# One core, fp32r matmuls in high and low parts: a merged matmul of 512 columns in the up pass, and sums of halves on VectorE

## The reference

```
u = rms_norm(h, norm_mlp_g)
h = h + square(relu(u @ w_mlp_up)) @ w_mlp_down     # w_mlp_up 2048 x 8192, w_mlp_down 8192 x 2048
out = rms_norm(h, norm_final_g)
```

## Time and profile before

| | |
|---|---|
| time, median of 3 runs | 2653.86 us (2652.83 to 2655.21) |
| profiled execution | 2654.28 us, its span 2652.6 us |
| PE busy | 98% |
| DVE, ACT, POOL busy | 63%, 44%, 17% |
| up pass, pairs 1 to 31 | 1386.9 to 2011.8 us |
| longest waits of PE in the up pass | one of 9.3 us at its start |

### The profile page before, as it was taken

How to read it: one execution, slowest core, us unless ns; L and a number is a source line. 1 busy time by engine, 2 the same in 40 slices (tenths; PEclk the granted TensorE clock), 3 DMA queues, 4 the chain that set the end, 5 groups by cost and what they waited for, 6 DMA issues and landing times. The chain is left out here.

```text
span 2652.6 us, 37285 instructions
## 1 busy us (share of the span) xinstructions
PE 2595.1 (98%) x14068; PEld 2253.3 (85%) x14068; DVE 1658.5 (63%) x1673; ACT 1154.6 (44%) x1437; POOL 460.9 (17%) x321
## 2 busy tenths in 40 slices
PE   7999999999999999999989999999999899999998
PEld 6888878888888888888879999999998788888886
DVE  5436844433233332342377788777878889999996
ACT  4333354312233322232355556556555455455555
POOL 1000010000000000000002223322332344344343
PEclk9999999999999999999989999999999999999999
DMA  5222322222322222234335565565568865545651
GB/s 173 92 82 80 107 87 97 95 95 80 95 79 79 80 95 95 95 111 137 132 111 179 195 216 183 183 211 198 178 199 323 242 242 203 174 181 217 237 206 80
DMA packets 247374, 394.39 MB, mean 149 GB/s; under 512 B 8832, under 2 KB 156880, under 8 KB 238864
## 3 DMA queue, kind: packets, MB, share of 16 engines
q1 hardware_dynamic: 240848, 373.97, 41.6%
q0 software_dynamic: 5520, 14.16, 2.1%
q10 hardware_dynamic: 944, 5.42, 0.5%
HBM read 326.28 MB, written 67.11 MB: 148 GB/s over the span
## 5 line engine op out<-in xcount | busy, mean ns | idle before, releaser
L1050 DVE TENSOR_TENSOR wlo<-raw,whi 128x2048 fp32r<-128x2048 f32 (+1 forms) x113 | 258.1, 2284 | 542.2 <-ACT whi L643 542.1
L1550 PE MATMUL stream<-uhi,whi 128*128 128x512 f32 (+1 forms) x1312 | 511.3, 390 | 0.8 <-ACT rx L715 0.8
L1551 PE MATMUL stream<-ulo,whi 128*128 128x512 f32 (+1 forms) x1312 | 507.7, 387 | 0.0
L1552 PE MATMUL stream<-uhi,wlo 128*128 128x512 f32 (+1 forms) x1312 | 507.4, 387 | 0.0
L643 ACT CAST whi<-raw 128x2048 fp32r<-128x2048 f32 (+1 forms) x113 | 215.3, 1906 | 534.9 <-PE stream L1552 533.9
L1550 PEld LDWEIGHTS stream<-uhi,whi 128*128 128x128 f32 (+1 forms) x1312 | 245.4, 187 | 52.6 <-issue 2.6
L1552 PEld LDWEIGHTS stream<-uhi,wlo 128*128 128x128 f32 (+1 forms) x1312 | 245.3, 187 | 50.3
L1551 PEld LDWEIGHTS stream<-ulo,whi 128*128 128x128 f32 (+1 forms) x1312 | 245.4, 187 | 49.5 <-issue 1.0
L605 POOL TENSOR_TENSOR hh<-hh,dn_tmp 128x512 f32<-128x512 f32 x116 | 221.5, 1929 | 352.5 <-ACT dn_tmp L969 352.5
L1818 PE MATMUL stream<-shi,uwhi 128*128 128x256 f32 x896 | 255.1, 285 | 9.3 <-DVE slo L1325 9.3
L1819 PE MATMUL stream<-slo,uwhi 128*128 128x256 f32 x896 | 254.7, 284 | 0.0
(11 more groups left out here) (258 smaller groups left out, 5142.0 us busy)
## 6 DMA issues: line engine op xcount, KB each, us to landing
raw<-in_w_in SPq DMA_DIRECT2D x80, 1024.0 KB, 5.1
d<-in_w_mlp_down SPq DMA_DIRECT2D x64, 1024.0 KB, 8.5
dsum<-sums_d SPq DMA_DIRECT2D x56, 1024.0 KB, 8.7
up_a<-in_w_mlp_up SPq DMA_DIRECT2D x32, 1024.0 KB, 6.3
up_b<-in_w_mlp_up SPq DMA_DIRECT2D x32, 1024.0 KB, 8.6
sums_d<-hhi SPq DMA_DIRECT2D x32, 896.0 KB, 6.0
sums_d<-hlo SPq DMA_DIRECT2D x32, 896.0 KB, 7.8
raw<-in_w_out SPq DMA_DIRECT2D x16, 1024.0 KB, 5.1
```

Of the source, the lines that this page charges most:

```text
L1050: V.tensor_tensor(wlo[slot][:, 0:width], raw[slot][:, 0:width], whi[slot][:, 0:width].bitcast(F32), ALU.subtract).then_inc(s.lo_ready, 1)
L1550: T.matmul(dst, ah, bh, start=first and k == 0, stop=False)
L1551: T.matmul(dst, ah, bl, start=False, stop=False)
L1552: ins = T.matmul(dst, al, bh, start=False, stop=last and k == n - 1)
```

## The change

The high and the low part of each activation sum now lie in one tile `ssum[q]` with a dimension of two. For each block the high weights are multiplied with both parts in one matmul of 512 columns into a whole bank: the left half gets high x high, the right half high x low. The low weights are multiplied with the high part, 256 columns, into the left half. So a state is now the sum of the two halves of its bank. ACT copies the right half (counted in `up_right`), and DVE adds the left half to the copy (the new function `whole`, counted in `up_snap`). `hid_out` adds the right half in a second operation that waits for the first (`up_half`). c21 is copied without relu, and ACT applies the relu in place in `hid_act`, ahead of the square, which waits for it.

The queue of DVE in a pair becomes: hid_out(0), add 0, whole(U3 of the pair before), uwlo 0, add 1, uwlo 1, hid_out(2), add 2, uwlo 2, whole(c21 of the pair before), uwlo 3, whole(P1), add 3, uwlo 4, whole(Q5), uwlo 5, whole(U2), uwlo 6, hlo.

```diff
 
     HALF = S // 2
     hs = [at(f"hs{k}", 190 + 7 * k, [P, 7, HALF], F32) for k in range(2)]
-    sum_at = [(112, 119), (126, 133), (176, 183), (48, 80), (56, 88), (64, 96), (72, 104), (32, 39)]
-    shi = [at(f"shi{k}", a, [P, 7, HALF], F32R) for k, (a, _) in enumerate(sum_at)]
-    slo = [at(f"slo{k}", b, [P, 7, HALF], F32R) for k, (_, b) in enumerate(sum_at)]
+    sums_near = {k: at(f"sums{k}", kb, [P, 2, 7, HALF], F32R) for k, kb in ((0, 112), (1, 126), (2, 176), (7, 32))}
+    sums_far = at("sums_far", 48, [P, 2, 4, 8, HALF], F32R)
+    ssum = [sums_near[k][:] if k in sums_near else sums_far[:, :, k - 3, 0:7] for k in range(8)]
+    shi, slo = ([v[:, c] for v in ssum] for c in range(2))
     up_a = [at("up_a0", 0, [P, 8, 256], F32), at("up_a1", 144, [P, 8, 256], F32)]
     up_b = [at("up_b0", 8, [P, 8, 256], F32), at("up_b1", 152, [P, 8, 256], F32)]
     up_e = at("up_e", 140, [P, 8, P], F32)
...
             i = 4 * g + u
             n = 7 * i
             _, _, _, _, parts = up_parts(u)
-            a, c = up_bank(u, 0)[:, 0:HALF], up_bank(u, 1)[:, 0:HALF]
-            a_old = up_bank(u + 1, 0)[:, 0:HALF]
+            a, c = up_bank(u, 0)[:, HALF:S], up_bank(u, 1)[:, HALF:S]
+            a_old = up_bank(u + 1, 0)[:, HALF:S]
             for j in range(7):
                 act.wait_ge(s.up_mm, n + j + 1)
                 if j == 1 and not first:
                     act.wait_ge(s.up_c, 3 * i)
-                    nc.scalar.copy(snap["U3"][:], a_old).then_inc(s.up_snap, 1)
+                    nc.scalar.copy(snap["U3"][:], a_old).then_inc(s.up_right, 1)
                 if j == 3 and not first:
-                    nc.scalar.activation(c21[:], a_old, ACT.Relu).then_inc(s.up_snap, 1)
+                    nc.scalar.copy(c21[:], a_old).then_inc(s.up_right, 1)
                 if j == 4:
                     act.wait_ge(s.up_c, 3 * i + 1)
-                    nc.scalar.copy(snap["P1"][:], a).then_inc(s.up_snap, 1)
+                    nc.scalar.copy(snap["P1"][:], a).then_inc(s.up_right, 1)
                 if j == 5:
                     act.wait_ge(s.up_c, 3 * i + 3)
-                    nc.scalar.copy(snap["Q5"][:], c).then_inc(s.up_snap, 1)
+                    nc.scalar.copy(snap["Q5"][:], c).then_inc(s.up_right, 1)
                 if j == 6:
                     act.wait_ge(s.up_c, 3 * i + 2)
-                    nc.scalar.copy(snap["U2"][:], a).then_inc(s.up_snap, 1)
+                    nc.scalar.copy(snap["U2"][:], a).then_inc(s.up_right, 1)
 
                 if j < len(hooks):
                     hooks[j]()
...
             act.wait_ge(s.up_c, 3 * i + 6)
             nc.scalar.activation(up_out[:, :, 0:HALF], up_out[:, :, 0:HALF], ACT.Relu).then_inc(s.up_relu, 1)
             act.wait_ge(s.up_snap, 5 * i + 5)
+            nc.scalar.activation(c21[:], c21[:], ACT.Relu).then_inc(s.up_relu, 1)
             if begun:
                 act.wait_ge(s.hs_add, 4 * i)
+            act.wait_ge(s.up_relu, 2 * i + 2)
             nc.scalar.activation(h21[:], c21[:], ACT.Square).then_inc(s.up_sq, 1)
-            act.wait_ge(s.up_relu, i + 1)
             if begun:
                 act.wait_ge(s.hs_sp[u % 2], 64 * g + 32 * ((u - 2) // 2 + 1))
             nc.scalar.activation(hraw[:, 0:7:3], up_out[:, :, 0:HALF], ACT.Square).then_inc(s.up_sq, 1)
...
                     act.wait_ge(s.dn_mm, 14 * st + m + 1)
                 if first and m == 1:
                     act.wait_ge(s.up_c, 3 * PAIRS)
-                    nc.scalar.copy(snap["U3"][:], up_bank(3, 0)[:, 0:HALF]).then_inc(s.up_snap, 1)
+                    nc.scalar.copy(snap["U3"][:], up_bank(3, 0)[:, HALF:S]).then_inc(s.up_right, 1)
                 if first and m == 3:
-                    nc.scalar.activation(c21[:], up_bank(3, 0)[:, 0:HALF], ACT.Relu).then_inc(s.up_snap, 1)
+                    nc.scalar.copy(c21[:], up_bank(3, 0)[:, HALF:S]).then_inc(s.up_right, 1)
                 if m == 2 and not first:
                     dn_out(g - 1 + n, 1 - n, 4)
                 if m == 4 and not first:
...
 
         def sum_lo(k):
             dve.wait_ge(s.st_hi, k + 1)
-            V.tensor_tensor(slo[k][:], hs[k % 2][:], shi[k][:].bitcast(F32), ALU.subtract).then_inc(s.st_lo, 1)
+            V.tensor_tensor(slo[k], hs[k % 2][:], shi[k].bitcast(F32), ALU.subtract).then_inc(s.st_lo, 1)
 
         def out_sums(i):
             dve.wait_ge(s.h_in, 16 * i + 16)
...
                     if not isinstance(n, int) or n:
                         dve.wait_ge(s.up_lo, n)
                     add(0, up_e[:], b11, b12)
+                    if not first:
+                        whole(i - 1, 4, u - 1)
                 if j == 1:
                     dve.wait_ge(s.up_b[u % 2], loaded)
                     dve.wait_ge(s.up_lo, n + 1)
...
                 if j == 2:
                     add(2, b12, b12, b22)
                 if j == 4:
+                    whole(i, 0, u)
                     dve.wait_ge(s.up_lo, n + 2)
                     add(3, up_e[:], b11, b21)
                 if j < len(hooks):
                     hooks[j]()
                 k = (7 * u + j) % 4
+                if j >= 5:
+                    whole(i, j - 4, u)
+                if j == 3 and not first:
+                    whole(i - 1, 6, u - 1)
                 dve.wait_ge(s.up_hi, n + j + 1)
                 V.tensor_tensor(uwlo[k][:], parts[j], uwhi[k][:].bitcast(F32), ALU.subtract).then_inc(s.up_lo, 1)
                 if j == 6 and not first:
...
 
         def hid_out(i, u, j):
 
+            dve.wait_ge(s.up_mm, 7 * i + 8 + j)
+            x, part, op = ((0, "P1", ALU.add), None, (1, "U2", ALU.subtract))[j]
+            b = up_bank(u, 3 + j)
+            dve.wait_ge(s.up_snap, 5 * i + {0: 1, 2: 4}[j])
             if j == 0:
-                dve.wait_ge(s.up_mm, 7 * i + 8)
-                dve.wait_ge(s.up_snap, 5 * i + 1)
                 dve.wait_ge(s.up_sq, 2 * i + 2)
-                V.tensor_tensor(up_out[:, 0, 0:HALF], up_bank(u, 3)[:, 0:HALF], snap["P1"][:], ALU.add).then_inc(s.up_c, 1)
-            else:
-                dve.wait_ge(s.up_mm, 7 * i + 10)
-                dve.wait_ge(s.up_snap, 5 * i + 4)
-                V.tensor_tensor(up_out[:, 1, 0:HALF], up_bank(u, 5)[:, 0:HALF], snap["U2"][:], ALU.subtract).then_inc(s.up_c, 1)
+            V.tensor_tensor(up_out[:, x, 0:HALF], b[:, 0:HALF], snap[part][:], op).then_inc(s.up_half, 1)
+            if j == 2:
                 V.tensor_tensor(up_out[:, 2, 0:HALF], snap["Q5"][:], snap["U3"][:], ALU.subtract).then_inc(s.up_c, 1)
+            dve.wait_ge(s.up_half, 2 * i + j // 2 + 1)
+            V.tensor_tensor(up_out[:, x, 0:HALF], up_out[:, x, 0:HALF], b[:, HALF:S], ALU.add).then_inc(s.up_c, 1)
+
+        def whole(i, k, u):
+
+            part = (snap["P1"], snap["Q5"], snap["U2"], None, snap["U3"], None, c21)[k][:]
+            dve.wait_ge(s.up_right, 5 * i + {0: 1, 1: 2, 2: 3, 4: 4, 6: 5}[k])
+            V.tensor_tensor(part, up_bank(u, k)[:, 0:HALF], part, ALU.add).then_inc(s.up_snap, 1)
 
         def hid_lo(i):
             dve.wait_ge(s.hs_hi, i + 1)
...
                     dve.wait_ge(s.dn_b21, 16 * st + 16)
                     dve.wait_ge(s.dn_lo, 14 * st + 3 + hf)
                     add(3, dn_e[hf][:], b11, b21)
+                if first and m in (1, 3):
+                    whole(PAIRS - 1, m + 3, 3)
                 dve.wait_ge(s.dn_hi, 14 * st + m + 1)
                 V.tensor_tensor(dlo[m % 7][:], parts[j], dhi[m % 7][:].bitcast(F32), ALU.subtract).then_inc(s.dn_lo, 1)
                 if first and m == 1:
...
                 pe.wait_ge(s.up_lo, n + j + 1)
                 if j in (2, 4, 5, 6):
                     pe.wait_ge(s.up_snap, 5 * i + {2: 1, 4: 3, 5: 2, 6: 4}[j])
-                dst = up_bank(u, j)[:, 0:HALF]
+                dst = up_bank(u, j)
+                both = dst[:].rearrange("p (c n) -> p c n", c=2)
                 opens = j in (0, 1, 3)
                 for q in range(KP):
-                    wh, wl, sh, sl = uwhi[k][:, q], uwlo[k][:, q], shi[q][:, j], slo[q][:, j]
-                    T.matmul(dst, wh, sh, start=opens and q == 0, stop=False, skip_group_check=not opens)
-                    T.matmul(dst, wh, sl, start=False, stop=False, skip_group_check=not opens)
-                    ins = T.matmul(dst, wl, sh, start=False, stop=q == KP - 1, skip_group_check=not opens)
+                    wh, wl, hl, sh = uwhi[k][:, q], uwlo[k][:, q], ssum[q][:, :, j], shi[q][:, j]
+                    if q:
+                        T.matmul(dst[:, 0:HALF], wl, sh, start=False, stop=False, skip_group_check=True)
+                    ins = T.matmul(both, wh, hl, start=opens and q == 0, stop=q == KP - 1, skip_group_check=True)
+                    if q == 0:
+                        T.matmul(dst[:, 0:HALF], wl, sh, start=False, stop=False, skip_group_check=True)
                 ins.then_inc(s.up_mm, 1)
 
         for u in range(4):
```

(4 more changed lines are left out.)

## The result

The changed kernel takes 2703.4 us in the median of four runs (2702.45 to 2704.29); the kernel before, on the same chip, 2653.35 us (2652.62 to 2655.21). The ratio is 1.0185 with a 95% interval of 1.0172 to 1.0198: 50 us slower, where 42 were forecast. The profiled execution has a span of 2701.7 us, 49.1 more than before.

What follows compares the result with a forecast made beforehand. TensorE (20.16 us per pair) and a DVE-ACT-POOL chain (20.2) were taken as near-equal bounds; the chain grows to 14.07 + 5.8 + 1.76 = 21.6, the up pass by 42.2, giving 2696 us, range 2667 to 2720.

Steps and rivals of the forecast that it cites:

- Two equal bounds: Up pass: TensorE's 20.16 us per pair and a chain of 20.2 have almost the same length; faster TensorE alone gains nothing.
- nothing in the chain waits for TensorE: Up pass, kernel before: the closed stretch from hlo to hlo, 20.22 us, contains no wait for TensorE.
- The merged matmul: TensorE: three 256-column matmuls become one of 512 and one of 256, 0.360 to 0.3474 us; 0.71 us less per pair.
- The new wait and its place: TensorE's product 6 waits for DVE's addition of U3's halves, queued behind add 0 of the next pair; some 2 us.
- tied to the chain: TensorE, after first stalling about 2 us for U3's addition, follows the chain and waits in every pair.
- The sum: Whole kernel: first hlo about 1397.6, thirty links of 21.6 us, up pass +42.2 us, median 2696 us.
- The down pass: Begins with a wait for weights by DMA and hides its own extra adds; 1 us if it did not.
- The chain, longer: Hlo to hlo: added DVE and ACT work starts POOL at 14.07, was 11.94; POOL 5.8, hhi 1.76; chain 21.6 us.
- (a): Rival, faster: POOL gets through in DVE's PSUM adds, chain 18.8 us, TensorE's 19.45 the bound, 2631 us; chance 0.08.
- (b): Rival, no change: POOL at 4.3 us, chain 20.16, or POOL begins later; 2649 to 2659 us; chance 0.05.
- (c): Rival: waits lower TensorE's clock, P1 5.5 us later, chain some 27 us, over 2800; 0.10 together with chain above 22.35.
- (d): Rival: merged matmul costs what two did, TensorE keeps 20.16 us, time as forecast; no chance given.

Runs made afterwards that it cites:

- 1: Kernel before with the merged 512-column matmul alone, right halves of the banks unread: 2653.92 us, ratio 0.9999.
- 6: Kernel before with the four sums of hidden activations moved from POOL to DVE: 2653.7 us, ratio 0.9996.
- 7: Kernel before with both the merged matmul (right halves unread) and the four sums moved from POOL to DVE: 2635.97 us, ratio 0.9928.
- 9: Changed kernel with the addition of P1's halves put behind the fourth sum of weights (add 3), not ahead of it: 2679.1 us, ratio 1.0090.
- 3: Changed kernel with the addition of U3's halves moved from behind add 0 to directly behind hlo, ahead of hid_out: 2705.96 us, ratio 1.0191.
- 2: Changed kernel with its 512-column matmul split again into two of 256, one into each half of the bank: 2702.75 us, ratio 1.0181.
- 4: Changed kernel without ACT's relu of c21 ahead of its square: 2703.43 us, ratio 1.0185.
- experiment 10: Changed kernel with the addition of P1's halves one step earlier, ahead of uwlo 3: 2719.88 us, ratio 1.0247.

## Why the prediction was right, point by point

**Two equal bounds**: shown by 1, 6 and 7. Each bound removed alone gives nothing; both together give 18.6 us. That nothing in the chain waits for TensorE held for the kernel before: in 1 the seventh uwlo, which TensorE's third product releases, starts 0.7 us earlier, and the last sum ends at +18.46 as before. In the changed kernel it no longer holds, as 9 shows.

**The merged matmul.** The saving in the stream was estimated at 0.71 us per pair; experiment 7 shows 20.16 - 19.58 = 0.58. The size is off by a fifth. By the Trainium skill ("TensorE: Matmul & The Clock Gate", Back-to-back issue gap), which gives 2.5 ns beside the columns as the gap of a single isolated matmul, an estimate would have been 0.14; the trace goes against it.

**The new wait and its place**: right, in 29 pairs, 1.5 us by the profile and 1.7 from start to start where "some 2 us" was said. With some 0.4 at product 2, which waits for P1, it makes up nearly all of the 2.16 us by which the link of 21.74 exceeds TensorE's 19.58. That it is a symptom and not the cause was implied ("tied to the chain") and is shown by 3: with a wait for P1 in its place the mean link is 21.81 us for 21.76.

**The sum.** The mean link from the first hlo (1398.50) to that of 2051.16 is 21.755 us, forecast 21.6: that is 4.7 us in 30 links. The first hlo was expected at 1397.6: 0.9 more. The pass then ends 8.4 us behind the last hlo, forecast 8.5. The up pass so gives +47.7 us for a forecast of 42.2. The down pass was put at nothing, and that is right: 143 us into it, behind its last wait, the two kernels are within 0.2 us of each other, and at its end still. (It does not begin with a wait for weights, as the prediction says; TensorE goes on at once, and its first wait comes 14.5 us later in both kernels.) The missing 1.4 us arise in the last 20 us of the kernel, where DVE scales the output and POOL another part of it. Before and after:

```profile
2638.58 2.48 DVE L1517 SCALAR_TENSOR_TENSOR hh<-hh,small,gfin 128x1024 f32<-128x1024 f32 x2
...
2683.13 4.73 POOL L626 TENSOR_TENSOR hh<-hh,gfin 128x1024 f32<-128x1024 f32 x2
2686.13 4.01 DVE L1537 SCALAR_TENSOR_TENSOR hh<-hh,small,gfin 128x1024 f32<-128x1024 f32 x2
```

Before, POOL had ended at 2638.47 when DVE began. In the experiments the same pair of operations takes 2.48 to 4.45 us, 2.48 in 2 and 6 and 3.51 in 1, so this part does not follow from the change as far as the runs show.

**The step that failed, though its number came out**: "The chain, longer". I added 0.60 us for ACT's c21 relu and its wait (measured 0.44) and 0.24 for TensorE's way to the copy of P1, and priced POOL's span as free between 5.26 and 6.52. Experiments 2, 3 and 4 show that in these ranges ACT's part costs nothing: POOL's first sum ends where DVE's queue lets it. The right working is DVE's queue up to the addition of Q5's halves at +15.24, then POOL's and TensorE's way to the seventh uwlo. The added work that counts is DVE's: 1.13 us up to add 2, and 0.34 each for the additions of c21 and P1, ahead of the border at which POOL gets through: 1.81 in all. They are not all seen in the link. In the kernel before, no addition from PSUM stood at this border, and the first sum ended only behind the sixth uwlo, at +15.27:

```profile
1616.62 1.22 DVE L1378 TENSOR_TENSOR uwlo<-up_b,uwhi 128x1024 fp32r<-128x1024 f32 x1
```

So it ends 0.65 us later now, and from its end to that of the last sum it is 0.88 us longer (4.07 for 3.19); together that is the 1.53 of the link. That the two workings gave nearly the same sum is chance, and only the second explains 9.

**The rivals.** (a) had the right mechanism in the wrong strength: POOL does get through in DVE's additions from PSUM, but not before. (b) did not occur. (c) occurred once in the changed kernel and in 15 pairs of experiment 10, and there it delayed P1's copy by 1.5 us, not by the 5.5 that the prediction put: the stretch ended sooner than two products. (d) is excluded by 7, where TensorE's pair takes 19.58 us and not 20.16; 2 alone could not tell, since (d) expected the same time.

What stays open: why the first sum does not get through at the border between add 3 and the fifth uwlo, although in one pair of the kernel before POOL and DVE took turns there.

## What to carry to other kernels

When an engine is busy for 98% of a pass, look for the closed chain of the others from one iteration to the next, and compare its length with that engine's work: if they are equal, a gain needs both. Price an operation added to a chain by moving it in a trial, not by its row: beside a wait for a shared resource, 0.4 us on ACT cost nothing, and one addition moved 1.1 us later gained 24. Short sums on two SBUF tiles beside a busy DVE were 4 times as long on POOL as on DVE, even when DVE was already the fullest engine but one.

## What the runs showed of the hardware

- POOL's operation on 128x256 floats takes 0.74 us alone and up to 3.3 us beside DVE's long operations with two inputs in SBUF. In four kernels the end of the first such sum stood fixed to 0.01 us against DVE's queue while its start moved by 0.6 us.
- Single short waits of TensorE in an otherwise full stream were followed by its lower clock: all 15 of 1.92 to 2.01 us in experiment 10, nine of 21 of 1.73 to 1.79 us in experiment 3, none of the 27 of 1.5 to 1.6 us in the changed kernel. The length alone does not decide: a wait of 2.65 us at the end of the changed kernel's pass and one of 2.17 in experiment 10 were not followed by it.
- A merged matmul of 512 columns saves in the stream 0.58 us over 56 triples, 10 ns each.
